# Five of the twelve modulation products of each layer move from the first block to the second block's neighbourhood phase and mixer

## The reference, cut to what matters

```
for l in range(DEPTH):                                  # DEPTH = 2
    sh1, sc1, g1, sh2, sc2, g2 = adaln(c, w_mod[l], b_mod[l], 6)      # silu(c) @ w_mod[l] + b_mod[l]
    ctx_mod = adaln(c_ctx, w_mod[l], b_mod[l], ...)
    hc = modulate(ctx, ctx_mod[0], ctx_mod[1]);  h = modulate(x, sh1, sc1)
    o_a = window_gqa_latent(...)                        # phases wa (and ca for the context)
    o_b = neighbourhood_latent(...)                     # phase nb (and cb for the context, layer 0)
    o_c = conformer_conv(...)
    o = concatenate([o_a, o_b, o_c]) @ w_out[l]         # the mixer
    x = layer_norm(ALPHA * x + g1 * o, ln1_g[l], ln1_b[l])
    h2 = modulate(x, sh2, sc2)
    x = layer_norm(ALPHA * x + g2 * ec_moe(h2, ...), ln2_g[l], ln2_b[l])   # 16 experts, each takes its top tokens
```

## Time and profile before

| | |
|---|---|
| median of 3 runs | 2793.3 us (2789.22 to 2798.05) |
| profiled execution, its own time | 2786.06 us |
| its span, first to last instruction | 2784.2 us |
| PE busy | 2620.4 us |
| mean granted clock of PE | 0.986 |
| moved by the transfer engines | 570.06 MB |

### The profile page before, as it was taken

The page is one execution under the profiler, slowest core; times in us unless marked ns, Lnnn a source line. Parts: engine busy times, 40 slices in busy tenths (PEclk is TensorE's granted clock), DMA queues, the critical chain, the costliest instruction groups (busy, mean ns, idle before and its releaser), DMA issues. The chain is left out here.

```text
span 2784.2 us, 44403 instructions
## 1 busy us (share of the span) xinstructions
PE 2620.4 (94%) x17914; PEld 1421.7 (51%) x17914; DVE 1069.5 (38%) x2323; ACT 698.4 (25%) x1835; POOL 207.4 (7%) x253
## 2 busy tenths in 40 slices
PE   8999999999999999898999999999999989999897
PEld 5565656565657766555434444436766543322222
DVE  3023340023447853656122222237752552332234
ACT  2125311134412443422111111203442320000000
POOL 2000020000001010011000000001010110000000
PEclk9999999999999999999999999999999999999999
DMA  8343634443632011025999999972012249999996
GB/s 246 88 123 90 181 88 121 121 124 78 205 75 55 31 29 31 31 91 217 380 377 399 399 395 396 404 210 63 16 29 91 106 184 398 404 410 411 404 413 272
DMA packets 268627, 570.06 MB, mean 205 GB/s; under 512 B 12416, under 2 KB 203200, under 8 KB 219328
## 3 DMA queue, kind: packets, MB, share of 16 engines
q1 hardware_dynamic: 256512, 528.69, 52.0%
q0 software_dynamic: 11824, 39.18, 5.3%
q10 hardware_dynamic: 144, 0.14, 0.0%
HBM read 551.53 MB, written 16.42 MB: 204 GB/s over the span
## 5 line engine op out<-in xcount | busy, mean ns | idle before, releaser
L510 PE MATMUL ps<-turned,ring 128*128 128x512 f32 (+1 forms) x880 | 327.6, 530 | 0.0
L510 PEld LDWEIGHTS ps<-turned,ring 128*128 128x128 f32 x880 | 166.4, 190 | 153.9 <-issue 147.7
L818 PE MATMUL ps<-ring,mixT 128*128 128x512 f32 x512 | 223.6, 594 | 0.8 <-DVE mixT L1993 0.8
L1423 ACT ACTIVATE work<-ps 128x512 f32<-128x512 f32 x32 | 19.1, 598 | 687.7 <-PE ps L1325 404.7
L2034 ACT ACTIVATE probsT<-ps 128x512 f32<-128x512 f32 (+3 forms) x280 | 120.5, 456 | 230.2 <-PE ps L646 143.8
L1967 DVE TENSOR_REDUCE col<-ps 128x1 f32<-128x256 f32 (+4 forms) x136 | 79.0, 581 | 257.5 <-PE ps L604 224.5
L604 PE MATMUL ps<-kz,qz 96*128 96x512 f32 (+3 forms) x320 | 135.9, 507 | 22.6 <-ACT probs_v L2021 10.0
L2021 ACT ACTIVATE probs_v<-ps,col 128x256 f32<-128x256 f32 (+5 forms) x216 | 136.5, 632 | 79.6 <-DVE col L1967 56.9
L818 PEld LDWEIGHTS ps<-ring,mixT 128*128 128x128 f32 x512 | 95.8, 190 | 114.6 <-issue 113.4
L553 PE MATMUL ps<-turned,ring 128*128 128x512 f32 (+1 forms) x352 | 152.8, 562 | 1.0 <-DMA ring<-in_w_in 1.0
L632 PE MATMUL ps<-const,probs_v 128*128 128x128 f32 x752 | 122.8, 280 | 17.0 <-DVE probs_v L1985 13.9
(11 more groups left out here) (327 smaller groups left out, 3976.4 us busy)
## 6 DMA issues: line engine op xcount, KB each, us to landing
ring<-in_w_gate SPq DMA_DIRECT2D x64, 1024.0 KB, 19.8
mixT<-in_w_up SPq DMA_DIRECT2D x64, 1024.0 KB, 14.1
ring<-in_w_mod SPq DMA_DIRECT2D x96, 512.0 KB, 5.6
ring<-in_w_up SPq DMA_DIRECT2D x48, 1024.0 KB
ring<-in_w_in SPq DMA_DIRECT2D x82, 512.0 KB, 6.4
turned<-in_w_gate SPq DMA_DIRECT2D x32, 1024.0 KB, 17.9
mixcT<-in_w_down SPq DMA_DIRECT2D x32, 1024.0 KB
probs_v<-in_w_down SPq DMA_DIRECT2D x32, 1024.0 KB
```

The source lines that it names most:

```text
L510: mm = nc.tensor.matmul(ps[:, b, 0:n], w[:, k, :], rhs[:, k, 0:n], start=(k == 0), stop=(k == KD - 1))
L818: mm = nc.tensor.matmul(ps[:, b, :], lhs[:, k, tl * P:(tl + 1) * P], w, start=(k == 0), stop=(k == KD - 1))
```

## The change

Of the 12 products of a layer, j 0 to 6 stay in the first block: fox, sb and mla at steps 0 and 2, and the one between the output tiles. The products at fox step 17, sb step 15, mla step 17 and mem steps 0 and 4 are taken out there. j 7 to 10 are woven into nb, j 11 stands in the mixer's tail in place of `pe_busy(pe, 3)`. Their slots move to `second_block_slots`. The scores of all phases but mla take 128 rows instead of 96, with zeros in the new ones. In the tails: the statistics of a tile's first half are taken before its second half, ACT copies the top values instead of DVE, POOL's scaling of the last tile is put behind the first gather, POOL's exchange of modulation rows stands in nb, and in the last layer the residual products come earlier with other banks, and ACT takes the statistics of tiles 1 to 3.

```
-        mod_order = [(l, j) for l in range(DEPTH) for j in range(12)]
+        FIRST_MODS, NB_MODS, LAST_MOD = 7, range(7, 11), 11
+        mod_order = [(l, j) for l in range(DEPTH) for j in range(FIRST_MODS)]
...
-            q = (QC if kind in ("ca", "cb") else qz)[0:KROWS, hh, t * P:(t + 1) * P]
+            R = slice(0, KROWS if kind == "mla" else P)
+            q = (QC if kind in ("ca", "cb") else qz)[R, hh, t * P:(t + 1) * P]
...
-        MOD_STEPS = {"fox": (0, 2, 17), "sb": (0, 2, 15), "mla": (0, 2, 17), "mem": (0, 4)}
+        MOD_STEPS = {"fox": (0, 2), "sb": (0, 2), "mla": (0, 2)}
...
+        def mod_products(l):
+            def products(fill):
+                def turn(j):
+                    pe_mod_turn(nc.tensor, (l, j))
+                    close_job_turned(("modT", l, j), fill["place"])
+                for j in NB_MODS:
+                    w = [slot(nc.tensor, ("mod", l, 4 * j + q)) for q in range(4)]
+                    job = ("mod", l, j)
+                    yield "not before", 1
+                    b = open_job(nc.tensor, job, keep=True)
+                    for k in range(KD):
+                        for q in range(4):
+                            mm = nc.tensor.matmul(ps[32 * q:32 * q + 32, b, 0:P], cond[:, k, :], w[q][:, k, :],
+                                                  start=(k == 0), stop=(k == KD - 1), skip_group_check=True)
+                        if k == KD - 1:
+                            mm.then_inc(*done("job_done", job))
...
+                            close_job(job, fill["place"])
+                        yield "ns", 280
+                        if k == 3 and j > NB_MODS[0]:
+                            turn(j - 1)
+                yield "not before", fill["place"][1] + 2
+                turn(NB_MODS[-1])
+            return products
...
+                    + [x for j in NB_MODS for x in mod_slots(l, j)]
+                    + [(w1(2 + l, "wo", k), w_rows(a["w_out_2"], l, k)) for k in range(KD)]
+                    + mod_slots(l, LAST_MOD))
...
-            pe_softmax(pe, ("nb", l, 0))
+            pe_softmax(pe, ("nb", l, 0), mod_products(l), 400)
...
                     if i == n:
-                        pe_busy(pe, 3)
+                        pe_mod(pe, (l, LAST_MOD))
+                    else:
+                        pe_mod_turn(pe, (l, LAST_MOD))
...
+                if half == 0:
+                    dve.wait_ge(*(at("evac_dve", job) if kind == "first" else at("dve_step", ("res", st, t, 0))))
+                    dve_half_stats(dve, (st, t), res(t))
...
             for i in range(len(us) + lag + 3):
...
+                for job in closed_at(ph, i - 1):
+                    if job[0] == "modT":
+                        dve_mod(dve, job[1:])
...
+            nc.scalar.activation(spare, total, ACT.Copy, accum_out=end_col(1, t)).then_inc(*done("act_step", ("sum", t)))
+            act.wait_ge(*at("act_step", ("sum", t)))
+            nc.scalar.activation(end_col(0, t), end_col(1, t), ACT.Copy, scale=-1.0 / D).then_inc(*done("act_step", ("mean", t)))
+            act.wait_ge(*at("act_step", ("mean", t)))
+            nc.scalar.activation(spare, total, ACT.Square, bias=end_col(0, t),
+                                 accum_out=end_col(2, t)).then_inc(*done("act_step", ("squares", t)))
...
+                    if last and t > 0:
+                        dve.wait_ge(*at("act_step", ("squares", t)))
+                        nc.vector.scalar_tensor_tensor(res(t), total, end_col(0, t), rows_of(st)[0], ALU.add,
+                                                       ALU.mult).then_inc(*done("dve_step", ("ce", (st, t))))
```

More of the change, by code:

```diff
@@ L600, in pe_scores @@
                     parts.append((unit16, causal16, w - P))
-                parts += [(q, KC[0:KROWS, part, c * P:(c + 1) * P], w + c * P) for c in range(NC)]
+                parts += [(q, KC[R, part, c * P:(c + 1) * P], w + c * P) for c in range(NC)]
             for lhs, rhs, o in parts:
@@ L1362, in body @@
                     gate(e + 1, 1 - odd)
+                last = l > 0 and is_number(e) and e == EXPERTS - 1
+                if last:
+                    residual(0, 0)
                 pe.wait_ge(*nth("hid", l, e))
@@ L1837, in dve_topk, with twice, act_top_values @@
                     dve.wait_ge(*at("dve_step", ("mr", l, g)))
+        def twice(i, R, top, n):
+            return topd[R, i, :].rearrange("p (a n) -> p a n", n=n), top[R, 0:n].unsqueeze(1).broadcast_to(
+                [R.stop - R.start, P // n, n])
+        def act_top_values(act, l):
+            act.wait_ge(*at("dve_step", ("mx", l, CAP // 8 - 1)))
+            for r in range(3 if l == 0 else 2):
+                ins = nc.scalar.activation(*twice(0, slice(32 * r, 32 * r + 32), topv, CAP if r < 2 else CAP_C), ACT.Copy)
+            ins.then_inc(*done("top_values", l))
         def dve_slots(dve, l):
[L1842 to L1846, removed]
             nc.vector.tensor_copy(*twice(1, slice(0, 32), topi, CAP))
-            nc.vector.tensor_copy(*twice(0, slice(32, 64), topv, CAP))
             ins = nc.vector.tensor_scalar(*twice(1, slice(32, 64), topi, CAP), float(GROUP), None, ALU.add)
             if l == 0:
-                nc.vector.tensor_copy(*twice(0, slice(64, 96), topv, CAP_C))
                 ins = nc.vector.tensor_scalar(*twice(1, slice(64, 96), topi, CAP_C), float(SEQ), None, ALU.add)
@@ L1934, in dve_moe_out, with end_col, act_end_stats @@
                     head_end(t)
+        def end_col(k, t):
+            return dup[:, k, t:t + 1]
+        def act_end_stats(act, t):
+            l = DEPTH - 1
+            b = last_banks(l, t)[0]
+            total = psflat[:, b * 512:(b + 2) * 512]
+            spare = turned[:, 0:D]
+            act.wait_ge(*combined(l, EXPERTS - 1, t))
+            nc.scalar.activation(spare, total, ACT.Copy, accum_out=end_col(1, t)).then_inc(*done("act_step", ("sum", t)))
[4 more added lines that the diff above has]
+                                 accum_out=end_col(2, t)).then_inc(*done("act_step", ("squares", t)))
+            act.wait_ge(*at("act_step", ("squares", t)))
+            nc.scalar.activation(end_col(1, t), end_col(2, t), ACT.Ln, scale=1.0 / D,
+                                 bias=epsc(LN_EPS_2)).then_inc(*done("act_step", ("lv", ("end", t))))
+            act.wait_ge(*at("act_step", ("lv", ("end", t))))
+            nc.scalar.activation(end_col(3, t), end_col(1, t), ACT.Exp, scale=-0.5).then_inc(*done("rstd", (("experts", l), t)))
         def act_moe_out(act, l):
@@ L1998, in dve_softmax @@
             lag = lag_of(ph)
-            for i in range(len(us) + lag + 2):
+            for i in range(len(us) + lag + 3):
                 if i < len(us):
@@ L2827, in _ @@
                         ml, j = next(mods)
-                        for q in range(4):
-                            load_slot(sp_, ("mod", ml, 4 * j + q), w_cols(a["w_mod_2"], ml, (4 * j + q) * P))
+                        for key, part in mod_slots(ml, j):
+                            load_slot(sp_, key, part)
                     else:
```

165 lines of the change are left out of this document (112 added, 53 removed).

## The result

The changed kernel takes 2829.66 us (median of 4 runs, 2828.44 to 2832.4) where the kernel before takes 2791.84 (2789.22 to 2798.05): a ratio of 1.0138, 95% interval 1.0121 to 1.0154. The profiled execution has a span of 2828.0 us, 43.8 more than before's 2784.2. The medians differ by 37.8 only, because the profiled execution of before was 6 us faster than its median and that of after stood at its own.

A forecast was written before the change was run, and what follows sets the result against it. PE bounds the first block's fox, mla and mem; nb is a loop through three engines. Terms -17.4 + 50 + 6 - 4.2 = +34 on 2793.3 gave 2827 us, range 2788 to 2845.

The forecast's parts named there:

- First block: Fox, sb, mla and mem: five products taken out per layer save 8.7 us a layer, -17.4 us in all.
- The banks: In nb, PE waits for two shared banks, 2.8, 2.8 and about 2 us; with the slices, +50 us.
- The slices: Products woven into nb: 0.24 us per slice, 0.3 with the switch of shape, partly in PE's idle time.
- Nb in all: Both layers' nb: +50 us for woven products and bank waits, +6 for the clock.
- the clock: In nb, more drops to the lower clock behind the 2.8 us waits: +6 us, between none and 16.
- twice the clock: Rival in nb: the clock drops behind most waits, costing 16 to 23 us instead of 6, up to 2844; chance 0.2.
- Tails: Mixer's last tile to the gather: half statistics, affinity scaling and copies save 2.1 us a layer, -4.2 in all.
- the half statistics: Mixer's last tile: half the statistics, 0.65 of 1.29 us, go off DVE's path.
- The scaling of the affinities: Mixer's tail: falls from 1.52 to some 0.4 us when POOL scales later, saving 1.1.
- 4 MB of weights later: Layer 1's experts' weights wait for the mixer's end; idle transfers take most of them: 0 us, at worst 2.
- The end: Last layer's final tiles: ACT takes 3.6 us a tile, DVE's last passes end as before: 0, between -2 and +2.
- 128-row scores: Scores of all phases but mla: 128 rows instead of 96 cost nothing, 0 us.

The follow-up runs named there:

- both first: Changed kernel with DVE's `leave` and the modulation's addition both moved to the start of its step in nb: 2777.82 us, ratio 0.9940 to the kernel before.
- leave first: Changed kernel with DVE's copy of the last pair's result (`leave`) moved to the start of its step in nb: 2783.73 us, ratio 0.9978 to the kernel before.
- the version in one piece: Changed kernel with nb's products issued whole, bank 7 for modulations and bank 6 for `pe_pv`: 2768.73 us, ratio 0.9909 to the kernel before.
- 128 rows alone: Kernel before with only the scores of all phases but mla taking 128 rows instead of 96, zeros in the new rows: 2789.7 us, ratio 0.9991.
- the kernel before with leave first: Kernel before with DVE's `leave` copy moved to the start of its step in nb: 2789.02 us, ratio 0.9989.

## Why the prediction was right

It was 2827 with 2829.7 measured, and the mechanism was the one it named. That the number is so close is in part luck, as terms below missed by more than the total did, in both directions. Point by point, against the profiled execution:

- **First block: forecast -17.4, measured -20.9** to nb's first scores. Mla gives 1.9 (forecast 2.0), sb 1.4 (0.8), fox 3.2 (2.5) and mem 5.0 (3.4) in layer 0. Layer 1 gives 10.1 instead of 11.6, so that the first block ends 21.7 earlier: in its sb the changed kernel has a stretch at the lower clock, four matmuls in 3.65 us that take 1.98 in the kernel before. In mem I took 2.09 for two units from the first unit on; in fact the first four scores need no transposes between them and stand within 2.5 us.
- **The banks: right in each place.** 2.8 and 2.7 us where I wrote 2.8 twice, 1.5 where I wrote about 2; 40.8 in all where the forecast's terms make 45 or so. The experiments show the cause: moving `leave` takes its twelve waits away, moving the addition the other six, and separate banks make both moves worthless.
- **The slices: mis-sized.** I took 0.3 us for a slice. The four gapless steps of both first are 15.05 where those of before are 12.67 less two idle times of 0.53, 11.61: 3.44 for eight slices and a transpose, some 0.41 to 0.43 a slice. For 64 slices that is 7 to 8 us more than I had.
- **Nb in all: forecast +56 with the clock, measured +67.7.** Besides the slices, the clock: the stretches of nb at the lower level are 10.2 and 17.1 us where before had 3.4 and 3.4. What that costs is seen in PE's busy time: the same instructions take 129.8 us in the two nb phases of leave first, at full clock, and 143.8 here, 13.9 more. The 6.8 us of before cost half their length by the same measure, 3.4, so some 10 us went there (an estimate), where I took 6. The clock fell seven times, each time within a microsecond of the end of one of the twelve waits of 2.7 to 2.9 us, and behind the other five it did not; no drop is left in either nb phase of leave first. My rival "twice the clock" named 16 to 23; the stated range reached 2845 and so held the upper end of that rival, which its own sentence leaves out.
- **Tails: forecast -4.2, measured some -1.8.** The stretches outside the first block and nb give 3.0 in all, of which the end, below, is more than half. From the mixer's tiles to the gather the delay falls by 1.0 in layer 0 and 0.8 in layer 1: the half statistics give their 0.6 a layer, and the copies 0.3. The scaling of the affinities fell from 1.52 to 0.23, as forecast, and this gave next to nothing: that step failed. PE's route products now wait for ACT's half of the head,

```profile
2304.76 2.49 PE L815 MATMUL ps<-wr,qz 128*128 128x16 f32 x16 [1.04 <-ACT qz L1864]
```

  From the mixer's last addition to the indices it is 28.25 us in layer 1 where it was 29.04: 0.8, not 2.1.
- **4 MB of weights later: forecast 0, wrong in its reason.** I said that most of them would find idle transfer engines. They were still being loaded when the gather came: in layer 0 the transfer share was 1.02 at its issue where it had been 0.10, it landed after 8.4 us where it had taken 4.2, and PE stood for it:

```profile
1338.04 1.55 PE L1327 MATMUL ps<-const,turned 96*128 96x96 f32 x8 [3.67 <-DMA turned<-x_norm,idx]
```

  The delay against before grew there from 11.0 us at the last tile's affinities to 15.0 at the first gate product and 15.7 at the second expert's; in layer 1 it grew from 45.6 to 47.1 at the first gate product. It came back by two other ways. In layer 1 the experts wait for weights anyway, PE 27.0 us in all before and 24.9 now, and the delay was 45.4 at their end. In layer 0 an idle time of the kernel before was gone, which I had not seen. Before, then after, at the second expert's products:

```profile
1408.31 1.08 PE L1325 MATMUL ps<-h,probsT 128*32 128x512 f32 x4 [3.76 <-issue]
```

```profile
1421.06 1.07 PE L1393 MATMUL ps<-h,probsT 128*32 128x512 f32 x8 [0.79 <-issue]
```

  "issue" is time for which the profile shows no releaser. All three profiles of the kernel before and its two variants have 3.7 or 3.8 us there, the changed kernel and its seven versions 1.0 or less; with the clock drop behind it, it took the delay from 15.7 to 11.4, 4.3 us. What sets it was not tried, and it is a part of the 23 us by which the version in one piece beats the kernel before that the moved products did not earn.
- **The end: forecast 0, measured -1.65.** From the last down product to DVE's last instruction it is 17.5 us where it was 19.2. ACT needs 3.04 a tile, not 3.6: its two passes take 1.01 and 1.11 where I took 1.2, and of its small steps one takes 0.29, the others 0.2:

```profile
2815.48 1.01 ACT L2048 ACTIVATE turned<-ps 128x1024 f32<-128x1024 f32 x1
2816.39 0.19 ACT L2048 ACTIVATION_READ_ACCUMULATOR turned<-ps 128x1 f32 x1
2816.61 0.20 ACT L2050 ACTIVATE dup<-dup 128x1 f32<-128x1 f32 x1
2816.84 1.11 ACT L2052 ACTIVATE turned<-ps,dup 128x1024 f32<-128x1024 f32 x1
```

- **128-row scores: 0, shown** by their own run.

The sum of the steps was +34 and the profiled executions differ by 43.8, so the forecast of the median was closer than its working, and by luck: I was 10 us low on the way, and 6 of these went because the profiled execution of before lay that much below its median, while that of the changed kernel lay at its own; I had taken the difference over unchanged.

What the weaving itself costs, apart from the banks: in one piece four steps take 13.92, of which 0.45 is idle, so 1.86 for a product with its transpose, against 3.44 in eight slices. The same matmuls cost 1.58 more when they are interrupted seven times, 0.11 for each of the 14 changes of shape more. The single rows say the same: in the changed kernel a slice starts 0.53 behind the start of the last scores where transposes start 0.43 behind it, and what follows a slice starts 0.36 behind it where an eighth of a whole product takes 0.24. The Trainium skill has a rule for this (TensorEngine Tiling (Array Packing), Key Properties): changing the tiling mode drains the engine. Between 128x128 and 128x32 the trace agrees, with that 0.11, though no run separates a drain from another cost of the change; between 96 and 128 rows the run with 128 rows alone shows no cost, 0.9991 of the time.

## What to carry to other kernels

Work woven into a loop takes more than engine time: it takes a bank, and a bank comes free at the last instruction of some other engine's step. Count, for each open, how many steps ago the bank's last user was made and where in the step its copy stands; give the woven work a bank of its own or move the copy to the front. Here whole products were better than slices (1.86 against 3.44 us each), as their shape differs from the loop's.

## What the runs showed of the hardware

Executions of one kernel differ in where the clock drops. In the kernel before with leave first, a product in fox ran at the lower clock:

```profile
199.16 0.46 PE L686 MATMUL ps<-hc,mixcT 128*128 128x128 f32 x2 [0.41 <-DVE modc L2116]
200.36 3.61 PE L553 MATMUL ps<-turned,ring 128*128 128x512 f32 x4 [0.74 <-DMA ring<-in_w_in]
```

In the run with 128 rows alone, which has the same instructions at this place, it did not, after 0.19 us less of idle time:

```profile
199.30 0.46 PE L687 MATMUL ps<-hc,mixcT 128*128 128x128 f32 x2 [0.41 <-DVE modc L2115]
200.30 1.98 PE L553 MATMUL ps<-turned,ring 128*128 128x512 f32 x4 [0.55 <-DMA ring<-in_w_in]
```

The drop costs 1.6 us here. The length of the idle time alone does not tell whether one comes: in sb of layer 1 PE stood for 1.39 and 1.36 us in the kernel before and in the changed one alike, and only the second had a drop behind it. The spread of the runs follows the clock. Of the 43 runs of the kernel before that stand beside the experiments, the shortest, 2781.05 us, has a mean granted clock of 0.990 and the longest, 2797.68, one of 0.982. That is a reason to read a change by its stages and not by the span of two profiles.

And a wait of PE costs more than its length where the clock falls behind it: the four steps from step 5 of layer 1, with 10.24 us at the lower clock, took 26.80 us, the next four, with 3.41 us of it and the same waits within 0.05 us, took 23.98.
